# A two-block transformer layer on one core: barriers behind two attentions, and work that is moved among their items

## Chip, core and metric

The kernel runs on one core of one Trainium2 chip. The metric is the device time of one execution in microseconds, the median of the runs. The engines are called PE (TensorE, matrix products), DVE (VectorE), ACT (ScalarE), POOL (GpSimd) and SP (SyncE, which here only issues DMAs). ACTq and SPq in rows are the instruction queues of ACT and SP issuing DMAs.

## The reference

Two blocks run one behind the other on x of 512 rows (tokens) and 1024 columns. The first has a mixer (retention and a chunked RWKV-7 scan side by side), a cross-attention on 256 rows of memory, and an MLP. The second has four attentions on shares of the width, and a feed-forward with a convolution, all scaled and shifted by a vector c. Cut to what the change touches:

```python
x = x + y @ w_out                                    # y: retention and RWKV-7
x = x + memory_cross_attention(rmsnorm(x, norm_xattn), rmsnorm(mem, norm_mem), w_q, w_kv, w_o)
x = x + jnp.square(jax.nn.relu(h @ mlp_w_up)) @ mlp_w_down
x = rmsnorm(x, norm_final)
# second block; mod = silu(c) @ ada_w + ada_b, cut into sh_a, sc_a, gt_a, sh_m, sc_m, gt_m
h = rmsnorm_2(x, norm_mix_g) * (1.0 + sc_a) + sh_a
proj = h @ w_in
# o_a: diff attention, rmsnorm_2(o, sub_g) * (1 - lam_init) behind it; o_b: forgetting attention
# o_c: stick-breaking attention; o_d: sparse attention of three branches, whose keys
#      d_ks (selected) and d_kw (window) are columns of proj of 64 each
mixed = jnp.concatenate([o_a, o_b, o_c, o_d], axis=-1) @ w_out_2
x = x + gt_a * mixed
x = x + gt_m * conv_ffn(rmsnorm_2(x, norm_ffn_g) * (1.0 + sc_m) + sh_m, ...)
```

## The kernel before

Every large product is computed in three passes. A weight chunk of up to 128x2048 numbers is loaded by SP into one of two raw slots; ACT casts it to a rounded high part (line 409) and DVE subtracts that from the raw to get the low part (line 412), in one of two slots for parts; PE then multiplies high by high, high by low and low by high (line 389). The left side is split in the same way, into `AH` and `AL`. All weights of the program form one stream, `STREAM`. On every engine a generator walks over the chunks (`product_steps` on PE, `evac_steps` on ACT and DVE), and `fill(dense, n)` advances it by n units, a unit being half of a 128x512 block or one narrower block: 12 products of 512 columns. When `evac_steps` comes to a chunk it first splits the weights of the next one. The smaller work of a stage is written by hand between such fills, so each engine's order is fixed by the code and engines meet only at semaphores. `stage_end` is a barrier of PE, ACT and DVE.

The order of the stages: the start (parameters, norm of x), the first products `w_in` with rotation and retention among them (`front1_*`), the inversion of 64x64 triangles for the scan (`invert_*`), the scan, `w_out`, query and key products, cross-attention, `w_o`, the MLP, the second input product `w_in_2` with stick-breaking, the sparse branch's preparation and the norms of queries and keys among it (`front_*`), the mixers (40 items of the diff, forgetting and sparse attentions), sub-norm, `w_out_2`, and the feed-forward.

What the change touches:
- At the start, ACT squares x (`squares_act`, line 615), POOL makes the root (lines 624 and 626) and DVE scales the rows (line 631).
- `skew_bias_act` (line 548) issues eight DMAs of 512 KB from DRAM to DRAM, on ACT's queue, among the first products. What they write is read by `load_bias_act` at about 996 us.
- Cross-attention is a pipeline of 16 items over DVE, ACT and PE. Barriers stand before and behind it. Behind it `split_y_act` and `split_y_dve` (lines 737 and 742) split all of `yT` in four steps; the first two chunks of `w_o` wait for two each.
- `w_in_2` has 13 chunks. The key columns of the selected branch are multiplied twice side by side (they have to stand in both halves of the partitions), and so are those of the window branch, in a chunk of their own with 24 products.
- `norms_*` brings the sum of squares of the diff tiles first, and then that of the forgetting (fox) tiles.
- Behind the mixers stand a barrier, the sub-norm (`subnorm_*`), the rows of the two gates (`gate_rows_*`, 16 scalings on DVE and 16 products on PE), a barrier, and the split of all of `yT`.

## Time and profile before

| | us |
|---|---|
| median of 3 runs (1749.3 to 1753.15) | 1750.53 |
| profiled execution | 1750.18 |
| its span | 1748.0 |
| PE busy in it | 1645.3 |
| DVE, ACT, POOL busy | 902.6, 661.4, 72.7 |
| chain that ended last, share of PE | 82% |
| mean granted clock of PE | 0.976 |
| PE waits in line 647 for DVE's rows, four times | 13.8 |
| PE waits in line 389 for low weights, five times | 13.5 |
| PE waits in line 389 for the low part of `yT`, twice | 11.0 |
| PE waits in line 2202 for ACT's squares | 4.7 |
| PE waits in the sub-norm and gate rows | 6.1 |
| PE waits in line 908 for the rotation, about 95 us | 0.9 |

How to read the rows below. A row of the timeline has the start and the duration in us, the engine, the line of the code, the operation, the tiles written and read, the shape, the count, and in brackets how long the engine stood idle before it and what ended that. A matmul's duration overlaps the next one's, so its pace is read from starts. A granted clock of 1.00 is the higher level of PE's clock, 2.4 GHz, and 0.50 the lower, 1.2 GHz. A row of a window has its bounds, its length, busy time and count for PE, PE's weight loads, DVE, ACT and POOL, then the granted clock, the DMA engines' share and GB/s.

### The profile page before, as it was taken

To read this page: it belongs to the slowest core of one execution; us is meant where nothing else is said; L and a number is where in the kernel's file an instruction comes from. 1 tells how busy PE (TensorE), PEld (TensorE's weight loads), DVE (VectorE), ACT (ScalarE), POOL (GpSimd) and SP (SyncE) were. 2 spreads that over 40 slices of the span, in tenths; PEclk is the share of its full clock that TensorE was granted. 3 is DMA by queue.
4 is the path that set the end of the run, shared out by engine and by line. 5 is a ranking of instruction groups with operands and counts; after the bars stand their busy time and mean duration, and the time that the engine had idled before them with its cause. 6 is when DMAs were issued, how large, how long until landed. Compare 5 with 4: busy or idle time off the path is not lost.

```text
span 1748.0 us, 26094 instructions
## 1 busy us (share of the span) xinstructions
PE 1645.3 (94%) x11261; PEld 1321.4 (76%) x11261; DVE 902.6 (52%) x1405; ACT 661.4 (38%) x987; POOL 72.7 (4%) x105
## 2 busy tenths in 40 slices
PE   6899989999998999999999899889787999999998
PEld 5766769977895778888888687666456788888887
DVE  5354576526443454545454644326774555555544
ACT  4225831243434254232331443544772422222220
POOL 1200100000000000000000200001400000000000
PEclk9999999999999999999999999997998999999999
DMA  6912220002350344545444331320001233323322
GB/s 204 263 54 60 64 81 4 4 28 95 96 163 31 124 156 135 199 139 179 159 169 166 114 78 49 78 92 25 1 1 49 72 97 97 97 97 97 96 85 84
DMA packets 152260, 169.50 MB, mean 97 GB/s; under 512 B 16264, under 2 KB 113154, under 8 KB 151762
## 3 DMA queue, kind: packets, MB, share of 16 engines
q1 hardware_dynamic: 143128, 152.10, 27.6%
q10 hardware_dynamic: 9018, 15.74, 3.1%
q8 instruction: 89, 1.46, 0.4%
q14 instruction: 25, 0.20, 0.0%
HBM read 163.60 MB, written 6.32 MB: 97 GB/s over the span
## 4 chain that ended last, share of the span: by engine, by line
PE 82%; DVE 6%; ACT 6%; POOL 2%; issue 2%; ACTq 2%; DMA 1%; DVEq 0%; POOLq 0%
PE ps L389 65%; PE ps L1265 4%; PE ps L1424 2%; DVE weights_low L412 1%; PE ps L2359 1%; ACT weights_high L409 1%; PE ps L2532 1%; PE ps L2347 1%; PE ps L1644 1%; PE ps L2370 1%; ACT sb_hT L2448 1%; POOL sb_hT L2489 1%; PE ps L908 1%; PE ps L920 1%; PE ps L2202 1%
## 5 line engine op out<-in xcount | busy, mean ns | idle before, releaser
L389 PE MATMUL ps<-left_high,weights_high 128*128 128x512 f32 x1024 | 409.4, 400 | 20.3 <-DVE weights_low L412 13.5
L412 DVE TENSOR_TENSOR weights_low<-sb_weights_raw,weights_high 128x2048 fp32r<-128x2048 f32 (+2 forms) x119 | 266.5, 2239 | 285.0 <-ACT weights_high L409 284.9
L389 PE MATMUL ps<-left_high,weights_low 128*128 128x512 f32 x1024 | 401.6, 392 | 0.0
L389 PE MATMUL ps<-left_low,weights_high 128*128 128x512 f32 x1024 | 401.5, 392 | 0.0
L409 ACT CAST weights_high<-sb_weights_raw 128x2048 fp32r<-128x2048 f32 (+2 forms) x119 | 222.4, 1869 | 345.6 <-PE ps L389 301.3
L389 PEld LDWEIGHTS ps<-left_high,weights_high 128*128 128x128 f32 x1024 | 193.3, 189 | 75.8 <-DVE weights_low L412 18.3
L389 PEld LDWEIGHTS ps<-left_high,weights_low 128*128 128x128 f32 x1024 | 193.1, 189 | 41.8
L389 PEld LDWEIGHTS ps<-left_low,weights_high 128*128 128x128 f32 x1024 | 193.6, 189 | 41.1 <-issue 1.7
L389 PE MATMUL ps<-weights_high,hidden_high 128*128 128x512 f32 x432 | 169.0, 391 | 0.0
L389 PE MATMUL ps<-weights_high,hidden_low 128*128 128x512 f32 x432 | 168.2, 389 | 0.0
L389 PE MATMUL ps<-weights_low,hidden_high 128*128 128x512 f32 x432 | 168.1, 389 | 0.0
L389 PE MATMUL ps<-weights_high,left_high 128*128 128x512 f32 (+2 forms) x352 | 118.8, 337 | 11.7 <-DVE left_low L742 11.0
L389 PE MATMUL ps<-weights_low,left_high 128*128 128x512 f32 (+2 forms) x352 | 117.5, 334 | 0.0
L389 PE MATMUL ps<-weights_high,left_low 128*128 128x512 f32 (+2 forms) x352 | 117.5, 334 | 0.0
L389 PEld LDWEIGHTS ps<-weights_high,hidden_low 128*128 128x128 f32 x432 | 81.1, 188 | 17.1
L389 PEld LDWEIGHTS ps<-weights_low,hidden_high 128*128 128x128 f32 x432 | 81.1, 188 | 16.6
L389 PEld LDWEIGHTS ps<-weights_high,hidden_high 128*128 128x128 f32 x432 | 81.1, 188 | 16.6
L389 PEld LDWEIGHTS ps<-weights_high,left_high 128*128 128x128 f32 x352 | 67.6, 192 | 21.2 <-issue 13.2
L1843 DVE TENSOR_TENSOR hidden_low<-sb_arena,hidden_high 128x512 fp32r<-128x512 f32 x54 | 37.4, 692 | 89.5 <-ACT hidden_high L1838 89.5
L389 PEld LDWEIGHTS ps<-weights_low,left_high 128*128 128x128 f32 x352 | 67.6, 192 | 6.8 <-issue 0.2
L389 PEld LDWEIGHTS ps<-weights_high,left_low 128*128 128x128 f32 x352 | 67.6, 192 | 6.5
L1265 PE MATMUL ps<-sb_arena 64*64 64x64 f32 x2048 | 63.8, 222 | 5.0 <-DVE sb_arena L1316 4.1
(382 smaller groups left out, 2062.7 us busy)
## 6 DMA issues: line engine op xcount, KB each, us to landing
sb_weights_raw<-in_w_in SPq DMA_DIRECT2D x25, 1024.0 KB, 5.3
sb_yT<-in_ada_w SPq DMA_DIRECT2D x24, 1024.0 KB, 5.2
sb_weights_raw<-in_ffn_w_up SPq DMA_DIRECT2D x44, 512.0 KB, 5.1
sb_weights_raw<-in_mlp_w_up SPq DMA_DIRECT2D x16, 1024.0 KB, 6.3
sb_weights_raw<-in_mlp_w_down SPq DMA_DIRECT2D x16, 1024.0 KB, 7.6
sb_weights_raw<-in_ffn_w_down SPq DMA_DIRECT2D x10, 1024.0 KB, 5.0
sb_weights_raw<-in_w_out SPq DMA_DIRECT2D x8, 1024.0 KB, 5.0
sb_weights_raw<-in_xattn_w_kv SPq DMA_DIRECT2D x8, 1024.0 KB, 5.1
```

What stands on the lines that cost most here:

```text
L389: last = nc.tensor.matmul(o, lhsT, rhs, start=b["first"] and i == 0, stop=b["last"] and i == len(pairs) - 1)
L409: nc.scalar.copy(h[:, 0:n], raw[:, 0:n]).then_inc(w_high, 1)
L412: nc.vector.tensor_tensor(l[:, 0:n], raw[:, 0:n], h[:, 0:n].bitcast(F32), ALU.subtract).then_inc(w_low, 1)
L908: nc.tensor.matmul(ps[:, 2 + n % 4, 0:w], KTt[b, p_, kt * P:(kt + 1) * P], QT[b, p_, kt * P:S], start=True, stop=True).then_inc(ret_scores, 1)
L920: last = nc.tensor.matmul(ps[64 * e:64 * e + 64, 6 + p_ % 2, kt * P:S], VR[:, kt, h * 64:(h + 1) * 64], SCO[:, (s - 2) % 3, e, 0:w], start ...
L1265: last = nc.tensor.matmul(ps[b, bank, c * 64:(c + 1) * 64], lhsT(b, u, c), rhs(b, u, c), start=True, stop=True)
L1424: last = nc.tensor.matmul(o_of(b), *own_pairs[i], start=i == 0, stop=i == len(own_pairs) - 1)
L1644: last = nc.tensor.matmul(ps[b, 6 + o % 2, q0:S], v_of(x), PT[0:m, buf, x, q0:S], start=grp["begins"] and x == 0, stop=grp["ends"] and x = ...
L1843: nc.vector.tensor_tensor(HIDL[part % 2][:, i, :], x, HIDH[part % 2][:, i, :].bitcast(F32), ALU.subtract).then_inc(ff_low, 1)
L2202: last = nc.tensor.matmul(ps[:, 2 + f, :], mat, SQ[:, f, :], start=True, stop=True)
L2347: nc.tensor.matmul(ps[:, j % 4, 0:it["w"]], l, r, start=True, stop=True).then_inc(mx_scores, 1)
L2359: last = nc.tensor.transpose(ps[0:m, 4 + e, i * P:(i + 1) * P], src[:, c0:c0 + m], ident)
```

## The change

- The squares of the first norm are computed by DVE; the loop is staggered by one tile.
- The eight bias DMAs are issued at the head of `invert_act` instead of among the first products. Several semaphores are merged; the waits keep their meaning.
- The barrier behind cross-attention is gone. `yT` is split by tile of 128x512 beside the items (`CROSS_SPLIT`), and `w_o` goes in halves of the contracted dimension: both column chunks of tiles 0 to 3, then both of tiles 4 to 7, with all eight banks of PSUM open.
- The keys of both branches come from one product of 128 columns; ACT copies the two halves apart, and two DMAs copy each into the other half of the partitions. The chunk of 24 products is gone; the fox chunks now come ahead of the diff chunks, and the norm sums are in that order too.
- The gate rows are turned by two transposes in `sparse_pe`, stored in DRAM and loaded back with a broadcast.
- Both barriers behind the mixers are gone. Four tiles of `yT` are split beside items 10, 12, 17 and 21; the square of the diff outputs stands at item 20, its two sums on PE at items 35 and 38, and the rest of sub-norm beside the first half of `w_out_2`, which takes tiles 2 to 5 first and then 6, 7, 0, 1.

```diff
+        def squares_dve(v, nm, t):
+            o = nm["at"] + t
+            nc.vector.tensor_tensor_reduce(out=nm["rows"][:, t, :], in0=nm["src"][:, t, :], in1=nm["src"][:, t, :],
+                                           scale=1.0, scalar=0.0, op0=ALU.mult, op1=ALU.add,
+                                           accum_out=stat[:, o:o + 1]).then_inc(squares_done, 1)
...
             swap_act(a, 0)
-            skew_bias_act(a)
...
         def invert_act(a):
-            a.eng.dma_start(GUP0, A["rwkv_g_up"][0, 0:P]).then_inc(gate_up_loaded, 16)
-            a.eng.dma_start(GUP1[0:32], A["rwkv_g_up"][0, P:P + 32]).then_inc(gate_up_loaded, 16)
+            a.eng.dma_start(GUP0, A["rwkv_g_up"][0, 0:P]).then_inc(front_loaded, 16)
+            a.eng.dma_start(GUP1[0:32], A["rwkv_g_up"][0, P:P + 32]).then_inc(front_loaded, 16)
+            skew_bias_act(a)
...
+        def in_halves(W, halves, rows_of, evac_of):
+
+            out_ = []
+            for half in halves:
+                for c0 in (0, 512):
+                    blocks = [by_token(0, 512, lambda k, t=t, half=half: rows_of(t)(half[k]), "dve", evac_of(t, c0), nk=4,
+                                       first=half is halves[0], last=half is halves[-1]) for t in range(NT)]
+                    runs = [half] if half[3] - half[0] == 3 else [half[0:2], half[2:4]]
+                    out_.append(dict(pieces=[kview(W)[:, r[0]:r[-1] + 1, c0:c0 + 512] for r in runs], nk=4, width=512,
+                                     blocks=blocks, by_k=len(runs) > 1))
+                out_[-2]["left"] = 4
+            return out_
+
+        def add_half(t, c0):
...
+                if n in beside:
+                    split_low_dve(v, beside[n])
...
+                if n in beside:
+                    a.wait_ge(sa_out_kept, base_out + beside[n] + 1)
+                    split_high_act(a, beside[n])
...
+        def split_high_act(a, k):
+            nc.scalar.copy(AH[:, k, :], yT[:, k, :]).then_inc(split_high, 1)
+
+        def split_low_dve(v, k):
+            v.wait_ge(split_high, v.count(split_high))
+            nc.vector.tensor_tensor(AL[:, k, :], yT[:, k, :], AH[:, k, :].bitcast(F32), ALU.subtract).then_inc(split_low, 1)
+
+        CROSS_SPLIT = {8: 0, 9: 1, 12: 2, 13: 3, 16: 4, 17: 5}
...
+        def two_keys(a, src, free, value):
+
+            upper, lower = slice(0, 64), slice(64, P)
+            nc.scalar.copy(QK[upper, 10, :], src[upper])
+            nc.scalar.copy(QK[lower, 11, :], src[lower]).then_inc(free, 1)
+            a.wait_ge(free, value)
+            a.eng.dma_start(QK[lower, 10, :], QK[upper, 10, :]).then_inc(keys_spread, 16)
+            a.eng.dma_start(QK[upper, 11, :], QK[lower, 11, :]).then_inc(keys_spread, 16)
...
-            chunk_of(w2((2564, 2692), (2692, 2756), (2692, 2756)), [
-                by_feature(0, P, h_tile, S, "act", act_copy_to(KV)), fcol(P, 10)]),
+            chunk_of(w2((2564, 2692), (2692, 2756), (2820, 2884)), [
+                by_feature(0, P, h_tile, S, "act", act_copy_to(KV)), by_feature(P, P, h_tile, S, "act", two_keys)]),
             chunk_of(w2((2756, 2820), (2884, 2960), (1536, 1540)), trow(0, 144, 768)),
             chunk_of(w2((2308, 2564)), [fcol(0, 8), fcol(P, 9)]),
-            chunk_of(w2((2820, 2884), (2820, 2884)), [fcol(0, 11)]),
-
+
+            chunk_of(w2((1024, 1280)), [fcol(0, 6), fcol(P, 7)]),
+            chunk_of(w2((768, 1024)), [fcol(0, 4), fcol(P, 5)]),
             chunk_of(w2((0, 256)), [fcol(0, 0), fcol(P, 1)]),
             chunk_of(w2((256, 512)), [fcol(0, 2), fcol(P, 3)]),
-            chunk_of(w2((768, 1024)), [fcol(0, 4), fcol(P, 5)]),
-            chunk_of(w2((1024, 1280)), [fcol(0, 6), fcol(P, 7)]),
             chunk_of(w2((512, 768)), trow(0, 256, 0)),
             chunk_of(w2((1280, 1536)), trow(0, 256, 256)),
         ]
@@ -2063,11 +2080,11 @@
...
-            columns_kept(a, 6)
+            store_gates_act(a)
+            columns_kept(a, 5)
...
+            for i, (tiles, SQ, n, kept) in enumerate(((QK[:, 4:8, :], SQ_FOX, 64, 7), (QK[:, 0:4, :], SQ_DIFF, 32, 9))):
+                columns_kept(a, kept)
+                if i == 0:
+                    a.wait_ge(nsa_normed, 2)
+                nc.scalar.activation(SQ, tiles, ACT.Square).then_inc(qk_squared, 1)
+                fill(dense, 3 - i)
+                nc.scalar.preload_act_table_set(LN_SET)
+                a.wait_ge(qk_sums, 2 + i)
+                nc.scalar.activation(SQ, ps[:, 2:6, :], ACT.Ln, bias=EPS6, scale=1.0 / n).then_inc(qk_ln, 1)
+                nc.scalar.preload_act_table_set(EXP_SET)
+                a.wait_ge(qk_ln, 2 + i)
+                nc.scalar.activation(SQ, SQ, ACT.Exp, scale=-0.5).then_inc(qk_rstd, 1)
...
+            split_weights(a, "act", w_in_2[6]["index"])
...
-        def subnorm_pe(pe):
-            pe.wait_ge(qk_squared, 4)
-            for f in range(2):
-                last = nc.tensor.matmul(ps[:, f, :], sum64, DSQ[:, f, :], start=True, stop=True)
-            last.then_inc(qk_sums, 1)
-            gate_rows_pe(pe, DIAG, 6)
-            gate_rows_pe(pe, DIAG_M, 4)
-
...
+        def turn_gates_pe(pe):
+
+            for i, m in enumerate((16, 40)):
+                nc.tensor.transpose(ps[0:KT, 6, 64 + i * P:64 + (i + 1) * P], MOD[:, m:m + KT], ident)
+
+        def keep_gates_dve(v):
+            nc.vector.tensor_copy(GATE_ROWS, ps[0:KT, 6, 64:64 + 2 * P]).then_inc(gate_rows, 1)
+
...
+        def load_gates_act(a, i):
+            a.wait_ge(gate_moved, 32)
+            a.eng.dma_start((GROW, GROW_M)[i], gate_dram[i:i + 1].to_broadcast([P, D])).then_inc(gate_moved, 16)
...
+        MIX_SPLIT = {10: 4, 12: 5, 17: 2, 21: 3}
+
+        def beside_mixers_act(a, n):
+
+            if n in MIX_SPLIT:
+                k = MIX_SPLIT[n]
+                if k < 4:
+                    a.wait_ge(mx_out_kept, k + 1)
+                nc.scalar.copy(Y_HIGH[:, k - 2, :], yT[:, k, :]).then_inc(split_high, 1)
+            if n == 20:
+                a.wait_ge(fox_bias, 2 * len(FOX_ITEMS))
+                a.wait_ge(mx_out_kept, 2)
+                nc.scalar.activation(DSQ, yT[:, 0:2, :], ACT.Square).then_inc(qk_squared, 1)
+                load_gates_act(a, 0)
+            if n in (36, 39):
+                f = (n - 36) // 3
+                a.wait_ge(qk_sums, 4 + f)
+                nc.scalar.copy(DSQ[:, f, :], ps[:, 6, :]).then_inc(qk_ln, 1)
+
+        def beside_mixers_pe(pe, n):
+            if n in (35, 38):
+                f = (n - 35) // 3
+                pe.wait_ge(qk_squared, 4)
+                pe.wait_ge(mx_out_kept, 5)
+                if f:
+                    pe.wait_ge(qk_ln, 4)
+                nc.tensor.matmul(ps[:, 6, :], sum64, DSQ[:, f, :], start=True, stop=True).then_inc(qk_sums, 1)
+
+        def beside_mixers_dve(v, n):
+            if n in MIX_SPLIT:
+                k = MIX_SPLIT[n]
+                v.wait_ge(split_high, v.count(split_high))
+                nc.vector.tensor_tensor(Y_LOW[:, k - 2, :], yT[:, k, :], Y_HIGH[:, k - 2, :].bitcast(F32),
+                                        ALU.subtract).then_inc(split_low, 1)
+
+        TMPG = view(4096, 512)
...
+        def mixed_rows_2(t):
+            tok = slice(t * P, (t + 1) * P)
+            return lambda k: (Y_HIGH[:, k - 2, tok], Y_LOW[:, k - 2, tok]) if 2 <= k < 6 else \
+                (AH[:, k, tok], AL[:, k, tok])
+
+        w_out_2 = in_halves(A["w_out_2"][0], ((2, 3, 4, 5), (6, 7, 0, 1)), mixed_rows_2, gated_a)
...
-            for t in range(NT):
-                a.wait_ge(x_loaded[t // 2], 16)
-                squares_act(a, NORM_1, t)
...
         def w_o_pe(pe):
-            closing_norm_pe(pe, product_steps(pe, w_o, 8), w_o, NORM_4)
+            dense = product_steps(pe, w_o, 8)
+            for s in (sa_shifted, sa_kept):
+                pe.wait_ge(s, pe.seen[s.name])
+            fill(dense, 12)
+            pe.wait_ge(sa_out_kept, pe.seen[sa_out_kept.name])
+            closing_norm_pe(pe, dense, w_o, NORM_4)
...
         def w_out_2_act(a):
-            closing_norm_act(a, evac_steps(a, "act", w_out_2), w_out_2, NORM_6, gated)
+            dense = evac_steps(a, "act", w_out_2)
+            fill(dense, 1)
+            load_gates_act(a, 1)
+            a.wait_ge(mx_out_kept, 6)
+            for k in (6, 7):
+                split_high_act(a, k)
+            nc.scalar.preload_act_table_set(LN_SET)
+            a.wait_ge(qk_ln, 5)
+            nc.scalar.activation(DSQ, DSQ, ACT.Ln, bias=EPS6, scale=1.0 / HD).then_inc(act_order, 1)
+            nc.scalar.preload_act_table_set(EXP_SET)
+            a.wait_ge(act_order, a.count(act_order))
+            nc.scalar.activation(DSQ, DSQ, ACT.Exp, scale=-0.5).then_inc(qk_rstd, 1)
+            for k in (0, 1):
+                a.wait_ge(sub_normed, k + 1)
+                split_high_act(a, k)
+            closing_norm_act(a, dense, w_out_2, NORM_6, gated)
             nc.scalar.preload_act_table_set(SILU_SET)
...
             mixers_pe(pe)
-            pe.stage_end()
-            subnorm_pe(pe)
-            pe.stage_end()
             w_out_2_pe(pe)
             pe_products(pe, ffn)
```

The order of ACT's instructions where the bias DMAs stood, before: the load of `in_ret_masks`, the four DMAs of the first swap (line 863), and behind them the split of the fourth chunk's weights.

```order
L470 COPY sb_arena<-ps 128x512
L1166 DMA sb_yT<-in_ret_masks 128x4096
L863 DMA sb_arena<-sb_arena 32x2048 x4
L548 DMA bias_skewed<-bias_vectors 128x1024 x8
L409 CAST weights_high<-sb_weights_raw 128x2048
L470 COPY sb_arena<-ps 128x512 x2
```

And at the start of the inversion, before; the four copies keep the first products of the inversion:

```order
L1203 ACTIVATE sb_arena<-sb_arena 32x512
L1292 DMA sb_hT<-in_rwkv_g_up 128x512
L1293 DMA sb_hT<-in_rwkv_g_up 32x512
L1296 COPY sb_arena<-ps 128x512 x4
L1301 COPY sb_arena<-ps 128x512 x20
```

The same two places after the change, first among the first products, then at the inversion.

```order
L472 COPY sb_arena<-ps 128x512
L1152 DMA sb_yT<-in_ret_masks 128x4096
L849 DMA sb_arena<-sb_arena 32x2048 x4
L409 CAST weights_high<-sb_weights_raw 128x2048
L472 COPY sb_arena<-ps 128x512 x2
L409 CAST weights_high<-sb_weights_raw 128x2048
```

```order
L1188 ACTIVATE sb_arena<-sb_arena 32x512
L1277 DMA sb_hT<-in_rwkv_g_up 128x512
L1278 DMA sb_hT<-in_rwkv_g_up 32x512
L549 DMA bias_skewed<-bias_vectors 128x1024 x8
L1282 COPY sb_arena<-ps 128x512 x4
L1287 COPY sb_arena<-ps 128x512 x20
```

The eight DMAs went from the place ahead of the weight split to the place ahead of the inversion's first copy.

PE behind its last mixer product (line 2370 before, 2389 after), before and after:

```order
L2359 MATMUL ps<-sb_consts,sb_hT 128x128 x4
L2370 MATMUL ps<-sb_hT,sb_arena 64x128 x8
L2695 MATMUL ps<-sb_arena,sb_consts 128x512 x2
L2681 MATMUL ps<-sb_arena,sb_consts 128x128 x16
L389 MATMUL ps<-weights_high,left_high 128x512
L389 MATMUL ps<-weights_low,left_high 128x512
L389 MATMUL ps<-weights_high,left_low 128x512
```

```order
L2378 MATMUL ps<-sb_consts,sb_hT 128x128 x4
L2389 MATMUL ps<-sb_hT,sb_arena 64x128 x8
L389 MATMUL ps<-weights_high,mixed_high 128x512
L389 MATMUL ps<-weights_low,mixed_high 128x512
L389 MATMUL ps<-weights_high,mixed_low 128x512
L389 MATMUL ps<-weights_high,mixed_high 128x512
```

The two sums now stand among the last items, the sixteen gate products are gone, and the first products read the tiles split among the items.

ACT in `w_in_2`, from the table load behind the logarithms of stick-breaking's second pair; `in_nsa_phi_w` is the load of the compression weights, and `128x1280` are exponentials, before and after:

```order
L2601 ACT_TABLE_LOAD
L409 CAST weights_high<-sb_weights_raw 128x1024
L470 COPY sb_arena<-ps 128x512 x2
L2578 ACTIVATE sb_arena<-sb_arena 128x1280
L2606 DMA sb_yT<-in_nsa_phi_w 64x32x64 x2
L409 CAST weights_high<-sb_weights_raw 128x2048
L2578 ACTIVATE sb_arena<-sb_arena 128x1280
L470 COPY sb_arena<-ps 128x512
L409 CAST weights_high<-sb_weights_raw 128x2048
```

```order
L2623 ACT_TABLE_LOAD
L409 CAST weights_high<-sb_weights_raw 128x2048
L472 COPY sb_arena<-ps 128x512 x2
L2600 ACTIVATE sb_arena<-sb_arena 128x1280
L2629 DMA sb_yT<-in_nsa_phi_w 64x32x64 x2
L409 CAST weights_high<-sb_weights_raw 128x2048
L2600 ACTIVATE sb_arena<-sb_arena 128x1280
L472 COPY sb_arena<-ps 128x512
L2604 COPY sb_yT<-ps 128x512
```

The first cast belongs to the chunk that PE works on next: the short one of 1024 columns before, a full one now. The cast behind the DMAs is that of the chunk behind it in both, and the cast that followed the copy comes later.

## Rows read from the trace of the kernel before

**Rows 1.** Page of before, part 1: busy us of each engine
```profile
PE 1645.3 (94%) x11261; PEld 1321.4 (76%) x11261; DVE 902.6 (52%) x1405; ACT 661.4 (38%) x987; POOL 72.7 (4%) x105
```

**Rows 2.** Timeline of PE at the start of `w_o`: start, duration, engine
```profile
570.85 0.51 PE L389 MATMUL ps<-weights_high,left_high 128*128 128x512 f32 x1 [4.83 <-DVE left_low L742]
...
574.80 0.40 PE L389 MATMUL ps<-weights_low,left_high 128*128 128x512 f32 x1
...
580.25 0.39 PE L389 MATMUL ps<-weights_low,left_high 128*128 128x512 f32 x1
```

**Rows 3.** Timeline of the first 22 us, and the x loads by line
```profile
10.93 1.06 ACT L615 ACTIVATE sb_arena<-sb_X 128x1024 f32<-128x1024 f32 x1 [8.28 <-issue]
...
17.44 0.75 DVE L631 TENSOR_SCALAR sb_arena<-sb_X,sb_stat 128x1024 f32<-128x1024 f32 x1 [0.71 <-POOL sb_stat L626]
...
21.20 0.47 PE L389 MATMUL ps<-left_high,weights_high 128*128 128x512 f32 x1 [1.55 <-DVE left_low L675]
...
L554 SPq DMA_DIRECT2D sb_X<-in_x x2: 422/442/463, 1.2 to 1.6; - x2
...
DMA to landing us min/median/max: 5.4/6.5/7.6
```

**Rows 4.** Line 881 on POOL (ns min/median/max), and one of its rows beside DVE
```profile
L881 POOL TENSOR_TENSOR sb_arena<-sb_arena x8: 1286/1476/3267, 46.3 to 90.7; 128x512 f32<-128x512 f32 x8
...
65.45 2.28 DVE L412 TENSOR_TENSOR weights_low<-sb_weights_raw,weights_high 128x2048 fp32r<-128x2048 f32 x1
...
65.60 3.27 POOL L881 TENSOR_TENSOR sb_arena<-sb_arena 128x512 f32<-128x512 f32 x1 [0.63 <-DVE sb_arena L871]
```

**Rows 5.** Timeline from 49 to 62 us, and one window (clock 0.56)
```profile
49.73 7.77 ACTq L548 DMA_DIRECT2D bias_skewed<-bias_vectors  x8
57.60 1.90 ACT L409 CAST weights_high<-sb_weights_raw 128x2048 fp32r<-128x2048 f32 x1 [11.34 <-issue]
...
61.88 0.79 PE L389 MATMUL ps<-left_high,weights_high 128*128 128x512 f32 x1 [5.36 <-DVE weights_low L412]
...
61.90:66.50 4.60, 4.60 (x12) 3.64 (x13) 4.39 (x5) 0.37 (x1) 2.56 (x2) 0.56 1.04 282
```

**Rows 6.** The bias DMAs' issues (ns min/median/max), and the inversion's first rows
```profile
L548 ACTq DMA_DIRECT2D bias_skewed<-bias_vectors x8: 505/664/1652, 49.7 to 56.9; - x8
...
55.52 1.98 ACTq L548 DMA_DIRECT2D bias_skewed<-bias_vectors  x3
...
250.48 0.45 ACTq L1293 DMA_DIRECT2D sb_hT<-in_rwkv_g_up  x1
252.01 0.58 ACT L1296 COPY sb_arena<-ps 128x512 f32<-128x512 f32 x1 [2.63 <-PE ps L1265]
...
252.72 0.69 DVE L1307 TENSOR_TENSOR sb_arena<-ps,sb_consts 128x512 f32<-128x512 f32 x1 [2.70 <-ACT sb_arena L1296]
```

**Rows 7.** Timeline of `w_in_2` with stick-breaking and norm sums
```profile
1091.90 1.97 ACTq L2606 DMA_DIRECT2D sb_yT<-in_nsa_phi_w  x2
...
1095.78 1.26 ACT L2578 ACTIVATE sb_arena<-sb_arena 128x1280 f32<-128x1280 f32 x1
...
1098.25 0.80 PE L389 MATMUL ps<-left_high,weights_high 128*128 128x512 f32 x1 [6.14 <-DVE weights_low L412]
1103.67 2.37 PE L2541 MATMUL ps<-sb_arena 128*64 128x512 f32 x16
...
1112.07 3.59 PE L2092 MATMUL ps<-sb_arena,sb_consts 128*128 128x512 f32 x8
...
1168.44 5.40 PE L2202 MATMUL ps<-sb_arena,sb_consts 128*128 128x512 f32 x8 [4.69 <-ACT sb_arena L2214]
```

**Rows 8.** Timeline behind the mixers, and the window of their last 78 us
```profile
1307.93 0.58 ACT L2463 COPY sb_yT<-ps 128x512 f32<-128x512 f32 x1 [0.76 <-PE ps L2370]
...
1329.31 0.76 PE L389 MATMUL ps<-weights_high,left_high 128*128 128x512 f32 x1 [6.12 <-DVE left_low L742]
...
1230.00:1308.00 78.00, 66.12 (x570) 40.97 (x566) 55.98 (x244) 57.57 (x210) 19.16 (x24) 0.98 0.01 2
```

223 lines of the change are left out of this document (99 added, 124 removed).

## The prediction

> **What bounds the kernel now.** I read the page first, then the waits of TensorE (PE), then the timeline round each long wait. PE is busy for 1645.3 of the 1748.0 us [rows 1], and most of that is the product loop of line 389, which issues a 128x512 product every 0.227 us at full clock, 2.4 GHz ((580.25 - 574.80) / 24), and about every 0.44 us with the clock at its lower level, 1.2 GHz: right behind a stall, from 570.85 to 574.80, ten took 3.95 us instead of 2.27 [rows 2]. So the span can shrink in three ways only: fewer PE instructions, shorter PE waits, less PE work at half clock. Work of VectorE (DVE), ScalarE (ACT) or the queues counts only where PE ends up waiting. Each term below is therefore a shift of PE's own timeline; the next product chunk follows behind every one of them, and apart from the places named the waits between are small.
>
> The span is 1748.0 us and the profiled execution 1750.18 us, so 2.2 us lie outside; the median of the runs, 1750.53, is the same within 0.02%. I subtract from 1750.2.
>
> **The start: squares on DVE.** Before, ACT issues the parameter loads first and squares x only from 10.93 us; four tiles of x later DVE ends at 18.19 and the first product starts at 21.20. The two halves of x were issued at 1.2 and 1.6 and landed after 5.4 and 7.6 us, at 6.6 and 9.2 [rows 3]. DVE's squares have no row; the nearest is its fused 128x512 operation, and by the step between sizes I estimate 1.2 us for 1024 elements. Four squares and four scalings from 6.6 us then end at about 15.0, 3.2 us earlier. But the chain goes through GpSimd (POOL), and POOL's 128x512 operation took 3.27 us beside a DVE subtraction that reads two tiles of SBUF, against 1.29 at its shortest [rows 4]. If POOL's two small operations of a tile are held in the same way while DVE squares the next one, a tile takes some 2.6 us instead of the 1.47 before, the rows end near 17.3 and 0.9 us is left. The Trainium skill, SBUF — State Buffer, section Who interferes with whom, says that a DVE instruction with two SBUF inputs contends with a GpSimd instruction that reads SBUF; by that rule alone the term would be -0.9, without it -3.2. Those rows of POOL agree with the rule. The bounds are -0.5 and -3.2; nearer to the blocked end I take **-1.5 us**.
>
> **Bias vectors: eight DMAs moved from the first products to the inversion.** ACT spends 7.77 us (49.73 to 57.50) issuing the eight `bias_skewed` DMAs; the weight split behind them starts only at 57.60, and PE stands 5.36 us until 61.88. Then it works at a granted clock of 0.56 over the next 4.6 us [rows 5]: nine products at 0.44 instead of 0.227, 1.9 us. A 0.9 us wait of the retention's first scores on the rotation (the DMAs of the swap share the queue with these eight) should go as well. The weights themselves had landed long before, so once ACT is free nothing is late next: split 1.9, subtraction 2.3, ready about 3 us before PE asks. Gain 8.2 us, at least 6.
>
> They are now issued at the head of `invert_act`, behind two gate loads that end at 250.93, and ahead of ACT's first copy at 252.01, which DVE awaits 0.1 us later [rows 6]. From there DVE runs its masks without a gap for 14 us, and PE waits for the last of them, so what delays the copy delays the stage one for one. One issue took 0.505, 0.664 or 1.652 us (least, median, most) [rows 6]; the last three, with the queue drained of the swap, took 1.98 together, 0.66 each. Eight of these are 5.3 us; ACT is free at 256.2, 4.2 us late. Bounds: eight at 0.505, 2.9 us, and the whole 7.77, 6.7 us. PE also sits idle longer and may do more of the next level at half clock, up to 2 us. I take **+4.5 us** (2.9 to 9). Together the move is worth **-3.7**.
>
> **Cross-attention to w_o: no barrier, halves.** PE's last attention product ends at 566.0; it stands 4.83 us, until the split of the first two tiles of yT (ACT, then DVE), and its first ten products take 1.7 us longer than at full pace [rows 2]: 6.5 us in all. After the change tiles 0 to 3 are split at items 8, 9, 12 and 13, the weights of the first chunk are ready as before, and 96 products (21.8 us) of the first half run before tiles 4 to 7 are needed, of which the last two take ACT and DVE some 5 us with the next weight split. So nothing is late next. Cost: one 0.6 us cast now stands ahead of ACT's last copy of turned weights, and the casts beside items 8 to 13 fall where DVE and ACT are mostly idle: 0.6. **-5.3 us** (3.5 to 6.5).
>
> **w_in_2: one chunk less, another order.** Removed: 24 products, 24 x 0.227 = 5.4 us. The order matters more. Before, the short dup chunk ends at 1092.1, and the next chunk's split stands on ACT behind two DMA issues that themselves wait for DVE's exponents; PE waits 6.14 us and then needs 5.4 us for 12 products that should take 2.7 [rows 7]. After the change the chunk at that place is a full one, so PE has 24 more products ready. It now reaches the stick-breaking times_v at 1094.8 and waits there for ACT's exponentials, which come behind the same two issues and the same split and end at 1097.05 [rows 7]: a new wait of 2.4 us, where before it got there at 1103.67. Net 6.4 us. Second, the sums of the norms: PE waited 4.69 us for the fox squares, which ACT reached only behind Ln of the diff tiles, a table load and a split, and ran the eight rows in 5.40 us instead of 3.59 [rows 7]: 6.5 us. Now both squares are placed right behind their columns, three units of products (8 us) ahead of PE's use, against 4.4 us of ACT work, so that wait goes. Two small waits of 0.3 and 0.2 shrink. Added on PE: two 8x128 transposes, 0.3. The two half-copies and two DMA issues of the shared product lie in ACT's idle time before the exponentials (4.3 us there); the gate stores cost ACT under 1 us, with PE's products ahead. Sum: 5.4 + 6.4 + 6.5 + 0.2 - 0.3 = **-18.2 us** (13 to 21).
>
> **Mixers to w_out_2: barriers, sub-norm and gate rows.** PE's last mixer product ends at 1307.9 and the first product of w_out_2 starts at 1329.31 [rows 8]: 21.4 us in which PE did 36 instructions of sums and gate rows. The first seven products run at half clock, 1.4 us more. After the change the four tiles of the first half are split by item 21, and PE goes on at once. The next things due are the second weight split (ready about 5 us after the last item, wanted after 10.9), the broadcast of the gate row (wanted after 24 us), and sub-norm with its two table loads, two functions, scaling and splits (some 12 us, wanted after 21.8). None is late, so the whole 22.8 us go.
>
> What is put in among the items costs something: PE gets two f32 128x512 sums, 0.9 each at full clock (3.59 / 4 [rows 7]); ACT gets four casts of 0.6, one square of 1.06 and two copies of 0.6; DVE four subtractions of 0.7. From 1230 on PE is busy 66 of 78 us, DVE 56 and ACT 58 [rows 8], each waiting for another by turns, so cover is thin. A split also ties DVE to ACT once, since the subtraction waits for a cast that stands behind ACT's copies; I estimate 1 us for each of the four (those at items 10 and 12 lie partly under POOL's bias work). 4 x 1 + 1.8 + 1 for the rest is nearly 7, less what is hidden: 6 us. Bounds 2 (the PE sums alone) and 12 (all of it serial, 1.8 + 4.7 + 2.8, and 2.7 of coupling). **-16.8 us** (11 to 21).
>
> **Sum.** -1.5 - 3.7 - 5.3 - 18.2 - 16.8 = -45.5, so 1750.2 - 45.5 = **1704.7 us**.
>
> **Rivals.**
> A. Waits come back in another place: the issues of the DMAs cost the inversion 9 us and DVE and ACT are coupled in the mixers for 12. For it: ACT stands directly on the chain at 252.01, and cover in the mixers is thin. Against: the issues were long only behind the swap. 1704.7 + 4.5 + 6 = 1715.2. Chance 0.2.
> B. The upper ends hold: starts at -3.2, inversion +2.9, mixers +2, front -20: 1704.7 - 1.7 - 1.6 - 4 - 1.8 = 1695.6. Chance 0.15.
> C. The change doesn't do what it says at w_out_2: the second waits put in (bank of the sums, kept outputs) or the first chunk's weights stop PE for as long as sub-norm takes. The order shows the products right behind the last times_v, and the first chunk's weights were there before the mixers, so this is unlikely. 1704.7 + 15 = 1719.7. Chance 0.06.
> D. The other side: half clock through the mixers. PE's clock was at its lower level for part of their first third. If waits among the items held it there from 1230 us to the end, the 66 us of PE work would take 0.44 / 0.227 as long, 62 us more: 1704.7 + 62 = 1767, slower than before. It decides once 74% of that stretch (46 us over 62) is at half clock. Against: the stretch is now granted 0.98 [rows 8], and two sums make PE fuller, not emptier. Chance 0.02.
> My forecast has 0.57.
>
> **The numbers.** The predicted time is that of the forecast, 1704.7. A measurement of this kernel can tell 0.2%, 3.5 us, from no change. A range for 8 in 10 takes in B and A with their neighbours: 1693 to 1719. Faster 0.97, same 0.01, slower 0.02.
>
> **What the profile after would show.** First product near 19.7 us, not 21.2; no wait of PE at the fourth chunk of w_in; ACT's first copy of the inversion some 4 us behind PE's gram products; w_o's first product right behind the last attention product; one wait of 2 to 3 us at the stick-breaking times_v and none at the norm sums; the first w_out_2 product right behind the last mixer product and a mixer stage 2 to 12 us longer. PE busy about 20 us lower. I am wrong if the inversion's copy is more than 7 us late, if DVE or ACT is the releaser of long PE waits in the mixers, or if a new wait on low weights stands in w_in_2.

## The result, and the profile after

The changed kernel took 1733.30 us, the median of four runs (1730.08 to 1741.98), against 1749.91 before. The ratio is 0.9905, 95% interval 0.9882 to 0.9928: 0.95% faster, where 1704.7 was forecast and 1693 to 1719 was the range. The direction was right, the size was not: 16.6 us instead of 45.5.

The profiled execution is the fastest of the four, 1730.08 us with a span of 1728.1, so the trace explains 19.9 us (1748.0 - 1728.1), and 3.2 us of the median lie outside it; an experiment below shows where. Part 1 of the page after, PE's line, against [rows 1]:

```profile
PE 1633.0 (95%) x11207; PEld 1313.1 (76%) x11207; DVE 903.3 (52%) x1404; ACT 660.5 (38%) x990; POOL 75.9 (4%) x105
```

PE's busy time fell by 12.3 us (about 20 were forecast), so only 7.6 of the 19.9 us gained are idle time, though waits of 5.4, 4.8, 6.1 and 4.7 us and two barriers were to go. To see where the rest stayed, I cut both timelines of PE at the first instruction of each stage. All are starts of PE rows, in us of the stage:

| stage, from its first PE product to the next one's | before | after | difference | forecast |
|---|---|---|---|---|
| start, up to the first product | 21.20 | 19.27 | -1.93 | -1.5 |
| first products, up to the inversion (rotation, retention) | 228.91 | 228.35 | -0.56 | -8.2 |
| inversion and scan, up to `w_out` | 133.14 | 138.56 | +5.42 | +4.5 |
| `w_out`, queries and keys of cross-attention | 144.86 | 144.86 | 0.00 | 0 |
| cross-attention, up to its last eight products | 32.51 | 36.46 | +3.95 | +0.6 |
| those products and `w_o`, up to the MLP | 61.26 | 54.61 | -6.65 | -5.9 |
| MLP and the norm behind it | 369.44 | 369.42 | -0.02 | 0 |
| `w_in_2` up to stick-breaking's second times_v | 112.35 | 105.78 | -6.57 | -6.4 |
| from there up to the mixers | 91.07 | 94.17 | +3.10 | -11.8 |
| mixers (before: with sub-norm and gate rows) | 134.57 | 119.44 | -15.13 | -15.4 |
| `w_out_2`, up to the feed-forward | 52.13 | 50.72 | -1.41 | -1.4 |
| feed-forward | 366.56 | 366.46 | -0.10 | 0 |

Two rows hold nearly the whole miss: the first products (7.6 us short) and the stretch from times_v to the mixers (14.9 us short). Cross-attention adds 3.4.

**The first products.** Against [rows 5] the weight split is no longer late; two other waits stand there. PE's timeline (columns as in that of before):

```profile
67.24 0.39 PE L389 MATMUL ps<-weights_high,left_high 128*128 128x256 f32 x1 [1.77 <-DVE weights_low L412]
...
77.42 0.58 PE L389 MATMUL ps<-weights_high,left_high 128*128 128x256 f32 x1 [4.16 <-ACT sb_arena L472]
```

ACT's timeline, with the casts, the second swap's issues and the copy:

```profile
47.26 1.91 ACT L409 CAST weights_high<-sb_weights_raw 128x2048 fp32r<-128x2048 f32 x1 [2.92 <-issue]
...
72.08 3.02 ACTq L849 DMA_DIRECT2D sb_arena<-sb_arena  x4
75.19 1.90 ACT L409 CAST weights_high<-sb_weights_raw 128x2048 fp32r<-128x2048 f32 x1 [9.10 <-issue]
77.00 0.64 ACT L472 COPY sb_arena<-ps 128x256 f32<-128x256 f32 x2
```

DVE's, with the first and last rotation row of the first swap and the weight subtraction between:

```profile
61.20 0.69 DVE L854 TENSOR_TENSOR sb_arena<-sb_arena 128x512 f32<-128x512 f32 x1 [9.70 <-DMA sb_arena<-sb_arena]
...
64.91 2.28 DVE L412 TENSOR_TENSOR weights_low<-sb_weights_raw,weights_high 128x2048 fp32r<-128x2048 f32 x1
...
70.39 1.60 DVE L857 TENSOR_TENSOR sb_arena<-sb_arena 128x512 f32<-128x512 f32 x1
```

The four DMAs of the first swap by line (what ACT spent on one issue in ns, the first and last start in us, the time to landing), after the change and before it:

```profile
L849 ACTq DMA_DIRECT2D sb_arena<-sb_arena x4: 612/614/860, 44.4 to 46.5; - x4
...
DMA to landing us min/median/max: 10.2/11.1/14.6
```

```profile
L863 ACTq DMA_DIRECT2D sb_arena<-sb_arena x4: 612/670/1025, 46.3 to 48.8; - x4
...
DMA to landing us min/median/max: 10.1/11.1/13.0
```

ACT now casts at 47.26 instead of 57.60. But DVE, free at 51.5, stands 9.70 us for the swapped tiles, whose DMAs were issued from 44.4 and landed only at 61. The next weight subtraction stands behind that rotation (64.91), which is PE's wait of 1.77 us; the second swap waits for the end of the rotation (72.0), ACT's copy that frees PE's bank stands behind it (77.00), and that is the wait of 4.16 us. Behind it, PE works some 6 us at half pace. Before, the last of the four landed 13.0 us after its issue at 48.8, so at 61.7, and DVE came free from the late split at 61.8: the landing was just as late as the split, and hidden by it.

**From times_v to the mixers.** The wait of 4.69 us of [rows 7] is gone; both sums start without one. A longer one stands further on. PE's timeline:

```profile
1176.82 0.55 PE L389 MATMUL ps<-weights_high,left_high 128*128 128x256 f32 x1 [11.74 <-DVE sb_arena L475]
```

ACT's, from the square of the diff tiles over the cast to the logarithm and the exponential:

```profile
1152.44 1.93 ACT L2233 ACTIVATE sb_yT<-sb_arena 128x2048 f32<-128x2048 f32 x1
1165.17 1.90 ACT L409 CAST weights_high<-sb_weights_raw 128x2048 fp32r<-128x2048 f32 x1 [10.80 <-PE ps L389]
...
1168.38 1.97 ACT L2237 ACTIVATE sb_yT<-ps,sb_eps 128x2048 f32<-128x2048 f32 x1
...
1171.66 1.91 ACT L2240 ACTIVATE sb_yT<-sb_yT 128x2048 f32<-128x2048 f32 x1
```

DVE's, with bank copies (line 475) and the scaling of the diff tiles (line 2248):

```profile
1155.16 0.75 DVE L475 COPY sb_arena<-ps 128x256 f32<-128x256 f32 x2
...
1173.60 1.41 DVE L2248 SCALAR_TENSOR_TENSOR sb_arena<-sb_arena,sb_derived_cols,sb_yT 128x512 f32<-128x512 f32 x2 [17.69 <-ACT sb_yT L2240]
1174.93 1.41 DVE L2248 SCALAR_TENSOR_TENSOR sb_arena<-sb_arena,sb_param_cols,sb_yT 128x512 f32<-128x512 f32 x2
1176.26 0.75 DVE L475 COPY sb_arena<-ps 128x256 f32<-128x256 f32 x2
```

The sums of the diff tiles are done at 1162.2. ACT doesn't take them, because its next instruction is the cast of the next weights, which waits 10.80 us, until PE at 1165.1 has used up the slot. The logarithm, the table load and the exponential follow, DVE's scaling waits for them 17.69 us, and DVE's two copies, which give PE its banks back, stand behind the scaling. PE, with two banks for its products here, has run out of them at 1165.1. The clock is at its lower level from 1168.5 to 1182.2, so the products of the first 5.3 us behind the wait run at half pace.

**What went as forecast.** times_v waits 2.27 us (2.4 forecast); no wait stands at the weights of the fourth chunk or at the norm sums; `w_o` and `w_out_2` start right behind their attentions, the latter at 1310.92, 18.4 us earlier than in [rows 8]:

```profile
1310.92 0.50 PE L389 MATMUL ps<-weights_high,mixed_high 128*128 128x512 f32 x1
```

### The profile page after: what moved, and what is told of

It reads as the page before. It is cut to its first block, busy times and chain, and to the rows that moved or that the text cites. A ratio compares the mean times of both kernels' runs of the same rounds, so it can differ in the third digit from the quotient of the medians.

```text
span 1728.1 us, 25989 instructions
## 1 busy us (share of the span) xinstructions
PE 1633.0 (95%) x11207; PEld 1313.1 (76%) x11207; DVE 903.3 (52%) x1404; ACT 660.5 (38%) x990; POOL 75.9 (4%) x105
## 4 chain that ended last, share of the span: by engine, by line
PE 82%; ACT 6%; DVE 6%; issue 2%; POOL 2%; ACTq 1%; DMA 1%; DVEq 0%; POOLq 0%; SPq 0%
PE ps L389 65%; PE ps L1250 4%; PE ps L1410 2%; PE ps L2378 1%; DVE weights_low L412 1%; ACT sb_hT L2469 1%; PE ps L2554 1%; PE ps L1636 1%; ACT weights_high L409 1%; PE ps L2366 1%; DMA sb_arena<-sb_arena 1%; PE ps L2389 1%; PE ps L894 1%; PE ps L906 1%; PE ps L381 0%
## 5 line engine op out<-in xcount | busy, mean ns | idle before, releaser
L389 PE MATMUL ps<-left_high,weights_high 128*128 128x512 f32 (+1 forms) x1016 | 404.1, 398 | 7.4 <-DVE left_low L693 3.2
L412 DVE TENSOR_TENSOR weights_low<-sb_weights_raw,weights_high 128x2048 fp32r<-128x2048 f32 (+1 forms) x118 | 265.3, 2248 | 263.1 <-ACT weights_high L409 263.1
L389 PE MATMUL ps<-left_low,weights_high 128*128 128x512 f32 (+1 forms) x1016 | 396.9, 391 | 0.0
L389 PE MATMUL ps<-left_high,weights_low 128*128 128x512 f32 (+1 forms) x1016 | 396.6, 390 | 0.0
L409 ACT CAST weights_high<-sb_weights_raw 128x2048 fp32r<-128x2048 f32 (+1 forms) x118 | 221.5, 1877 | 349.5 <-PE ps L389 294.1
L389 PEld LDWEIGHTS ps<-left_high,weights_high 128*128 128x128 f32 (+1 forms) x1016 | 190.6, 188 | 60.9 <-issue 13.7
L389 PEld LDWEIGHTS ps<-left_high,weights_low 128*128 128x128 f32 (+1 forms) x1016 | 190.8, 188 | 41.4
L389 PEld LDWEIGHTS ps<-left_low,weights_high 128*128 128x128 f32 (+1 forms) x1016 | 190.9, 188 | 40.4 <-issue 1.7
L389 PE MATMUL ps<-weights_high,left_high 128*128 128x256 f32 (+2 forms) x320 | 107.8, 337 | 19.4 <-DVE sb_arena L475 13.1
L389 PE MATMUL ps<-weights_low,left_high 128*128 128x256 f32 (+2 forms) x320 | 106.1, 331 | 0.0
L389 PEld LDWEIGHTS ps<-weights_low,hidden_high 128*128 128x128 f32 x432 | 81.1, 188 | 16.6
L389 PEld LDWEIGHTS ps<-weights_high,hidden_high 128*128 128x128 f32 x432 | 81.1, 188 | 16.5
L389 PEld LDWEIGHTS ps<-weights_high,left_high 128*128 128x128 f32 x320 | 63.2, 198 | 27.3 <-issue 12.6
```

What stands on the lines that cost most here:

```text
L389: last = nc.tensor.matmul(o, lhsT, rhs, start=b["first"] and i == 0, stop=b["last"] and i == len(pairs) - 1)
L409: nc.scalar.copy(h[:, 0:n], raw[:, 0:n]).then_inc(w_high, 1)
L412: nc.vector.tensor_tensor(l[:, 0:n], raw[:, 0:n], h[:, 0:n].bitcast(F32), ALU.subtract).then_inc(w_low, 1)
```

## The experiments

Each is the changed kernel with one thing altered, unless said otherwise. Medians of these kernels scatter by 3 us for a reason that the run of the unaltered kernel shows, so where a stage is at stake I read its length in the trace. Diffs are against the changed kernel. Five of the expectations also give a span, counted from the first trace of the changed kernel, and all five came out 3.5 to 11 us too low: 6.4 to 6.6 us of each miss lie in the mixers, which those edits don't touch.

### The swap ahead of the masks

```diff
-            a.eng.dma_start(DECAY, A["ret_masks"]).then_inc(front_loaded, 16)
             swap_act(a, 0)
+            a.eng.dma_start(DECAY, A["ret_masks"]).then_inc(front_loaded, 16)
```

> The changed kernel with one step moved: ACT issues the four DMAs of the first swap ahead of the 2 MB load of the retention masks instead of behind it. Theory 1 (the swapped tiles land late because they stand behind 2 MB on the same queue, and DVE's rotation, which waits for them, holds the weight subtraction and the second swap): the swap lands within 8 us instead of 11 to 15, DVE's rotation starts near 53 us instead of 61.2, PE's waits of 1.77 us (67.2) and 4.16 us (77.4) go, with 1.5 us of half clock behind the second, so the first product of line 990 comes 6 to 7.5 us earlier than at 168.0 and the span is near 1721. Rival (the swap is slow because the weight loads of SP take the DMA engines): landing stays over 11 us, and the gain is under 1 us.

Measured: 1728.88 us, ratio 0.988 (0.9865 to 0.9895). The first product of line 990 (the RWKV-7 branch, later in the same stage) came at 161.02 instead of 167.98, and no wait over 0.8 us stands between the first product and it. The landing of the first swap by line:

```profile
L849 ACTq DMA_DIRECT2D sb_arena<-sb_arena x4: 613/616/1187, 45.9 to 47.8; - x4
...
DMA to landing us min/median/max: 3.1/4.1/4.9
```

And the first row of DVE's rotation in the timeline, now without a wait:

```profile
54.49 0.69 DVE L854 TENSOR_TENSOR sb_arena<-sb_arena 128x512 f32<-128x512 f32 x1
```

The slowest of the four landed after 4.9 us instead of 14.6. The rival, SP's weight loads, falls with the next two runs, which have the bias DMAs back and differ in this order alone: SP issued no load in either between 39.1 and 59.7 us, and the four landed after 10.1 to 12.7 us behind the 2 MB load and after 3.1 to 5.0 ahead of it. So the 2 MB load ahead of the swap on the same queue was the cause, and theory 1 holds; only the last 2 us or so of the 14.6, where SP issued a load at 51.5, are not separated. The Trainium skill, DMA: Bandwidth & Descriptors, section Queues, rings and completion order, says that on each DMA engine the descriptors of one queue are consumed in ring order; the runs agree, 14.6 against 4.9 us. It is no order of landing: in the changed kernel the 2 MB load landed at 55.3 us, and the first of the four DMAs behind it at 54.6.

### The bias DMAs back among the first products

```diff
             swap_act(a, 0)
+            skew_bias_act(a)
             fill(dense, 8)
...
-            skew_bias_act(a)
             for u in range(NPAIR):
```

> The changed kernel with the eight bias DMAs issued where the kernel before had them, behind the first swap among the first products. Theory 3 (the move was worth almost nothing at the first products, because the rotation behind the landing of the swap was late right behind the weight split, and cost 5.4 us at the inversion): PE's 5.4 us wait for the fourth chunk's weights is back, but the first product of line 990 comes within 1 us of 168.0, the inversion's DVE masks start 5.4 us earlier behind its first product, and the span is 5 us shorter, about 1723. Rival (as predicted blind: 8.2 us gained at the first products against 5.4 at the inversion): 2.8 us longer, about 1731.

Measured: 1732.99 us, ratio 0.9889 (0.9867 to 0.9911). Both theories were wrong in part. The first product of line 990 came at 172.90, so the move was worth 4.9 us there, not under 1 and not 8.2; the inversion was 133.13 us, 5.4 shorter, as both said. The two cancel: the first mixer product comes at 1191.09 against 1191.48. The kernel before, with the same order of the DMAs, lost less: from the first product to that of line 990 it took 148.88 us, this run 153.70. The second row below has a part of it: the second swap, whose DMAs landed after 6.0 to 11.6 us (4.6 to 8.9 before; the bias DMAs, which there landed up to 76.5 us, stand ahead of it), lets DVE start at 88.15 instead of 86.44, and PE's wait for the rotation is 3.14 us instead of 0.86. PE also had 10.2 us at the lower clock level in this stage against 6.8. What is left of the 4.8 us is open.

PE's timeline:

```profile
61.16 0.57 PE L389 MATMUL ps<-left_high,weights_high 128*128 128x512 f32 x1 [4.99 <-DVE weights_low L412]
...
97.89 1.13 PE L894 MATMUL ps<-sb_arena 64*128 64x512 f32 x4 [3.14 <-DVE sb_arena L857]
```

### The swap ahead, and the bias DMAs back

```diff
-            a.eng.dma_start(DECAY, A["ret_masks"]).then_inc(front_loaded, 16)
             swap_act(a, 0)
+            a.eng.dma_start(DECAY, A["ret_masks"]).then_inc(front_loaded, 16)
+            skew_bias_act(a)
...
-            skew_bias_act(a)
             for u in range(NPAIR):
```

> As e1_swap_ahead_of_masks, but with the eight bias DMAs issued among the first products again, behind the swap and the masks. Theory 3: with the swap out of the way, the price of the eight issues at that place is what the forecast took for it, 7 to 8.5 us to the first product of line 990 (161.0 in e1, so 168 to 169.5), while in the changed kernel, where the swap was late, it was 4.9 (168.0 against 172.9). Rival (ACT's split was never the cause): under 4 us. The inversion is 5 to 6 us shorter in either case, so the span is within 3 us of that of e1.

Measured: 1732.11 us from two runs, ratio 0.9892 (0.9867 to 0.9918). The product of line 990 came at 167.99, 6.97 us after that of the run with the swap ahead alone; PE's wait for the split is there (5.27 us), and none for the rotation. So the forecast's 8.2 us was nearly the right price for the eight issues at that place, but it could be earned only once the swap was out of the way. The inversion took 134.06 us, 5.0 shorter.

### The bias DMAs where ACT waits anyway

```diff
             for f in range(4):
                 fill(dense, 1)
                 decays_act(a, f)
+            for f in range(4):
+                fill(dense, 1)
+                skew_bias_act(a, (2 * f, 2 * f + 1))
             fill(dense, 62)
...
-            skew_bias_act(a)
             for u in range(NPAIR):
```

> The changed kernel with the eight bias DMAs issued in pairs behind four of the last products of the first stage (about 215 to 240 us), where ACT waits 4 to 6 us for PE between its copies, instead of at the head of the inversion. Theory 3: the inversion stage (first product of line 1250 at its start to the first product of w_out) is 5.4 us shorter, 133.1 instead of 138.6, and nothing is longer before it; the span falls by 5.4. Rival (4 MB of DRAM traffic or the issues delay a weight chunk, PE waits for weights near 230 us): the stage before grows by 1 us or more.

Measured: 1727.65 us, ratio 0.9872 (0.9845 to 0.9898). The issues fell between 215.8 and 221.3 us, ahead of a wait of ACT for PE of 3.8 us; the stretch they are in, from line 990 to the inversion, kept its 79.6 us, and the inversion stage went from 138.56 to 134.31. That is 4.3 of the 5.4 us; ACT's first copy is as early as before, but PE had 12.9 us at the lower clock level in that stage against 10.2 before. The rival is out.

### The chain of the diff norms, on ACT alone and on both engines

```diff
-                fill(dense, 3 - i)
+                fill(dense, 3 if i == 0 else 0)
...
-                fill(dense, 5 if i == 0 else 0)
+                fill(dense, 5 if i == 0 else 2)
```

The second kernel has in `norms_dve` also `fill(dense, 4 - 2 * i)` for `fill(dense, 2)`.

> The changed kernel with one step moved on ACT: the two units of products that stood between the square of the diff tiles and the logarithm of their sums now stand behind the exponential. Theory 2 (PE's wait of 11.74 us at 1176.8 is the root chain of the diff norms: ACT waits 10.8 us for PE to free the weight slot, with the cast ahead of the logarithm; DVE's scaling waits for ACT, and the bank copies that PE needs stand behind the scaling): the logarithm starts right behind the sums at about 1162.3, DVE's scaling ends near 1170, and PE's wait falls from 11.7 to 4 to 6 us; span 1721 to 1723. Rival (the bank copies are late for DVE's own reasons, or the cast moved back becomes the new wait): PE's wait stays within 2 us of 11.7, or a wait as long appears at the first product of w_out_2.

> As e2_norm_act, and DVE takes two more units (four instead of two) between the scaling of the fox tiles and that of the diff tiles. Theory 2: PE now has two more banks to write while the chain of the diff norms runs (5.8 us of products), so no wait over 1 us is left before the mixers; the stage gives 13 us (the two waits of 1.3 and 11.7) and about 1 us of half clock, span 1714 to 1716. If the waits were only moved, the first mixer product comes less than 8 us earlier than at 1191.5.

Measured: 1727.97 us, ratio 0.9874 (0.9859 to 0.9888), and 1725.43, ratio 0.9857 (0.9841 to 0.9873). In the first, the logarithm in ACT's timeline and PE's wait:

```profile
1161.45 1.97 ACT L2237 ACTIVATE sb_yT<-ps,sb_eps 128x2048 f32<-128x2048 f32 x1 [6.58 <-PE ps L2224]
```

```profile
1169.90 0.55 PE L389 MATMUL ps<-weights_high,left_high 128*128 128x256 f32 x1 [5.62 <-DVE sb_arena L475]
```

PE's wait in the second:

```profile
1174.23 0.39 PE L389 MATMUL ps<-weights_high,left_high 128*128 128x256 f32 x1 [1.97 <-DVE sb_arena L475]
```

The wait fell from 11.74 to 5.62 and to 1.97 us, and the stage from 94.17 to 87.18 and 85.12. So both links are shown: the cast ahead of the logarithm, and the bank copies behind the scaling. Of the 13 us expected 9 came: waits of 1.30 and 1.97 us are left, since DVE's subtraction of the next weights also stands ahead of the copies, and here PE had half clock behind times_v.

### The subtractions one item later, in both attentions

```diff
-            attention_dve(v, cross, SRX, {n: k for n, k in CROSS_SPLIT.items() if n <= 16})
+            attention_dve(v, cross, SRX, {n + (n < 16): k for n, k in CROSS_SPLIT.items() if n <= 16})
```

> The changed kernel with DVE's four subtractions for tiles 0 to 3 of yT in cross-attention one item later than ACT's casts (items 9, 10, 13 and 14 instead of 8, 9, 12 and 13). Theory 4 (the attention stage grew from 32.5 to 36.5 us because each subtraction makes DVE wait 1.0 to 1.6 us for a cast that stands behind ACT's copies, and the next item's probabilities come late by that): DVE's waits for the casts go, the two PE waits of 1.82 us shrink below 0.8 us, and the stage from the first product of line 1613 to the last of line 1636 is 2 to 3 us shorter. Rival (the work put in is itself too much for ACT, four casts of 0.6 us): no more than 0.7 us.

Measured: 1728.47 us, ratio 0.9876 (0.9856 to 0.9895). The stage took 34.07 us instead of 36.46, and what was waited for in it (total, times, longest) in the changed kernel and in this one:

```profile
DVE left_low L1803 <- ACT left_high L1799: 6.7, 5, 1.6
PE ps L1624 <- DVE sb_arena L1690: 4.9, 5, 1.8
```

```profile
DVE left_low L1803 <- ACT left_high L1799: 1.9, 3, 1.5
PE ps L1624 <- DVE sb_arena L1690: 1.3, 3, 0.8
```

The price of the splits in cross-attention was 3.95 us, and 2.4 of it was the tie of DVE to ACT. The same edit in the mixers:

```diff
-            if n in MIX_SPLIT:
-                k = MIX_SPLIT[n]
+            if n - 1 in MIX_SPLIT:
+                k = MIX_SPLIT[n - 1]
```

> The changed kernel with DVE's four subtractions among the mixers one item later than ACT's casts. The stage (first mixer product to first product of w_out_2) was 119.4 us in the profiled run of the changed kernel and 125.8 to 125.9 in four of its variants, with more of it at the lower clock level. Theory 4: each subtraction costs DVE a wait of 1.3 us as at 1258.9, so the stage is 2 to 4 us shorter at the same clock pattern (about 122.5 where it would be 125.8). Rival (the cost is the casts and sums themselves): under 1 us.

Measured: 1732.36 us, ratio 0.9884 (0.9863 to 0.9906); the stage 122.75 us, granted clock 0.83. Kernels with the mixers unaltered had 124.7 us at 0.85 and 125.8 to 126.0 at 0.81 (below), so 0.83 would be near 125.3, and the edit is worth some 2.5 us by an estimate that leans on the clock. The best version, with this edit, had 117.9 at 0.90 against the changed kernel's 119.4 at 0.89; some 1.1 of these 1.6 us go to the clock by the slope of 6.6 us for 0.08 (below), and 0.5 is left. So the edit is worth 0.5 to 2.5 us by estimate. What the trace does show is that the waits are gone. DVE's subtractions and what they waited for in the changed kernel:

```profile
L2747 DVE TENSOR_TENSOR mixed_low<-sb_yT,mixed_high x4: 692/693/746, 1239.7 to 1270.0; 128x512 fp32r<-128x512 f32 x4
...
  ACT mixed_high L2723: 4.4, 4
```

Four waits, 4.4 us in total; with the edit there is none. How much of that reached PE is not settled.

### The changed kernel once more

> The changed kernel itself, unaltered, once more. Its runs lay between 1730.1 and 1742.0, and the stage from the first mixer product to w_out_2 was 119.4 us in its profile but 125.8 to 126.0 in five variants that touch nothing there. Theory 5 (the clock that the mixers are granted varies from run to run; the first profile caught a favourable one): the stage is over 122 us in this profile, with more than 27 us of it at the lower level, and the median stays at 1731 to 1735. Rival (the variants' edits upstream cause it): 119.4 again, with 27 us at the lower level.

Measured: 1736.97 us (1732.34 to 1737.90), ratio 0.9915 (0.9894 to 0.9936). The mixers in before (to their last product, without sub-norm), in the first profile of the changed kernel, and in this one (window, length, busy time and count of PE, its weight loads, DVE, ACT and POOL, granted clock, DMA):

```profile
1194.70:1308.00 113.30, 96.67 (x728) 59.30 (x728) 80.91 (x336) 80.06 (x282) 26.57 (x32) 0.89 0.01 1
```

```profile
1191.50:1310.90 119.40, 100.43 (x732) 61.03 (x732) 83.98 (x340) 83.85 (x288) 26.66 (x32) 0.89 0.02 6
```

```profile
1193.00:1319.00 126.00, 108.59 (x733) 66.50 (x733) 83.87 (x340) 84.00 (x288) 26.98 (x32) 0.81 0.02 5
```

Same instructions, same busy time of DVE and ACT, 6.6 us longer, at a granted clock of 0.81 instead of 0.89. PE was granted the lower level for 47.8 us of this stretch against 27.3. So the clock of this stage is not fixed by the program. The stage came out as theory 5 expected. The median didn't: 1736.97 us against an expected 1731 to 1735. The eight runs of this kernel lie between 1730.08 and 1741.98 us. Of the nine profiles in which nothing in the stage was altered, six had 0.81 and 125.8 to 126.0 us; the others had 0.85 (124.7), 0.87 (121.3) and 0.89 (119.4). The first trace was the most favourable of the nine, and the 3.2 us between it and the median are of this size and kind. What tips it is not shown. Nor is it shown whether the change has a part in it: of before there is one trace, at 0.89, but 29 of its 32 runs lie between 1747.7 and 1752.3 us, closer together than those of the changed kernel.

### All edits together

> All edits together: the swap ahead of the masks, both steps of the norms, the later subtractions in both attentions, the bias DMAs behind the last products of the first stage. If the theories hold and the gains add: 7 + 9 + 3 + 5.4 + 2 = 26 us under the 1733 of the changed kernel's median, 1703 to 1709. If they only move the waits, over 1715.

Measured: 1703.40 us, ratio 0.9725 (0.9708 to 0.9741). The gains add. Cumulative in the trace (of the slowest run, 1710.39 us, with the mixers at 0.83): the inversion starts 8.1 us earlier than in the changed kernel, `w_out` 13.0, cross-attention's end 15.4, the mixers 22.6.

One more step, in stick-breaking:

```diff
             weights(1, 0)
-            for i in range(2):
-                a.wait_ge(st_arg, 4)
-                a.eng.dma_start(PHI[...], ...).then_inc(prep_loaded, 16)
-            fill(dense, 1)
             weights(1, 1)
+            fill(dense, 1)
+            for i in range(2):
+                a.wait_ge(st_arg, 4)
+                a.eng.dma_start(PHI[...], ...).then_inc(prep_loaded, 16)
```

> As e8_all, and in the stick-breaking attention ACT takes the second exponential of the second pair at once, then the cast of the next weights, and then issues the two loads of the compression weights, which stood ahead of both. Theory 6 (PE's wait of 2.4 us at line 2563 is two DMA issues and a cast ahead of an exponential whose input is ready): the wait goes, the stage from w_in_2 to that product is 103.5 us instead of 106.1, and 1.5 us of half clock behind it goes too; median 1699 to 1701. Rival (the cast or the loads become late): the wait stays at over 1 us in another line within 20 us, 1703.

Measured: **1701.11 us** (1698.80 to 1706.09), ratio 0.9722 (0.9695 to 0.9749), the lowest median here. The runs overlap with those of the version above (1702.11 to 1710.39), so what the step is worth is read from the trace: the wait at times_v is gone, and the stage took 103.48 us instead of 106.08. The stretch behind it took 82.09 instead of 85.27, with no time at the lower clock level instead of 6.8 us.

### The splits behind the mixers

On the version above, `w_out_2_dve` having its four subtractions at its head likewise:

```diff
-        MIX_SPLIT = {10: 4, 12: 5, 17: 2, 21: 3}
+        MIX_SPLIT = {}
+        MIX_TILES = (4, 5, 2, 3)
...
         def w_out_2_act(a):
             dense = evac_steps(a, "act", w_out_2)
+            for k in MIX_TILES:
+                nc.scalar.copy(Y_HIGH[:, k - 2, :], yT[:, k, :]).then_inc(split_high, 1)
```

> As e10_all_and_stick, but the four casts and four subtractions of the split stand behind the mixers, ahead of the first half of w_out_2, and not among the items. What stays among them are the square, two sums, their two copies. Forecast's price (1 us for each of the four splits, 1.8 for the sums): first to last mixer product 4 us less than the 117.9 of e10 at the same clock reading of 0.90 (113.9; at a reading of 0.81 6.5 us more), and then a wait of PE of about 4 us for the splits: four casts of 0.6, the last subtraction and the next weight split. Rival (the splits hide among the items and the sums on PE are the price): the mixers are less than 1.5 us shorter.

Measured: 1703.48 us, ratio 0.9742 (0.9723 to 0.9762). The mixers with and without the splits, and PE's wait behind them:

```profile
1163.30:1281.20 117.90, 99.55 (x732) 59.69 (x732) 84.05 (x340) 83.37 (x288) 26.41 (x32) 0.90 0.02 6
```

```profile
1159.20:1276.40 117.20, 101.39 (x732) 61.64 (x732) 80.67 (x336) 81.55 (x284) 26.29 (x32) 0.87 0.02 6
```

```profile
1280.15 0.47 PE L389 MATMUL ps<-weights_high,mixed_high 128*128 128x512 f32 x1 [3.78 <-issue]
```

0.7 us shorter as it stands, but at a clock reading of 0.87 instead of 0.90. By the slope of the pair above (6.6 us for 0.08) that is 2.5 us, so by this estimate the splits cost about 3 us among the items, between the 4 of the forecast and the rival's 1.5. They save the wait of 3.78 us behind them, for which the profile names no releaser; ACT's four casts and DVE's four subtractions stand there, up to 1280.1 us. In the medians (1703.48 and 1701.11 us, with runs that overlap) the two places are level.

## Why the prediction was wrong, step by step

In the trace 25.6 us of the forecast's 45.5 are missing: 7.6 at the first products, 14.9 between times_v and the mixers, 3.4 in cross-attention; the other stages came within 1 us each.

**Start: right.** 1.93 us came where 1.5 (0.5 to 3.2) was forecast. What decided it is POOL's root, which takes 1.4 us beside DVE's squares and 0.55 without them. POOL's timeline, then DVE's squares:

```profile
8.78 0.55 POOL L633 TENSOR_TENSOR sb_stat<-sb_stat,sb_eps 128x1 f32<-128x1 f32 x1
...
10.25 1.42 POOL L633 TENSOR_TENSOR sb_stat<-sb_stat,sb_eps 128x1 f32<-128x1 f32 x1
...
12.59 1.41 POOL L633 TENSOR_TENSOR sb_stat<-sb_stat,sb_eps 128x1 f32<-128x1 f32 x1
```

```profile
10.04 1.22 DVE L621 CUSTOM_DVE_ANT_0 sb_arena<-sb_X 128x1024 f32<-128x1024 f32 x1
...
12.37 1.22 DVE L621 CUSTOM_DVE_ANT_0 sb_arena<-sb_X 128x1024 f32<-128x1024 f32 x1
```

A tile takes 2.3 us while squares are left (10.25 to 12.59), near the 2.6 that the forecast had for the blocked case, and a square took 1.22, as estimated. The rule of the Trainium skill, SBUF — State Buffer, section Who interferes with whom, holds here: a DVE instruction with both inputs in SBUF (here the same tile) delayed one of GpSimd that reads SBUF, by 0.87 us (1.42 - 0.55).

**Bias DMAs at the first products: the step "once ACT is free nothing is late next" failed.** The forecast asked only whether the weights had landed. It looked past DVE, where the subtraction stands behind a rotation that waits for the swap. The row was there to be found, in the trace of before: its first swap landed up to 13.0 us after the issue, the last of it at 61.7 us, as late as the stall that was to go. The late landing and the second swap behind it took 7.6 of the 8.2 us. With the swap ahead, 7.0 us came back.

**Inversion: right.** The eight issues took 5.99 us (5.3 forecast, 4.0 to 7.8 the bounds). The 0.66 us for one was read from issues "with the queue drained of the swap", which it wasn't: they fell at 55.5 to 56.9, and the swap landed up to 61.7. ACT's copies and DVE's masks followed:

```profile
248.46 5.99 ACTq L549 DMA_DIRECT2D bias_skewed<-bias_vectors  x8
254.49 2.05 ACT L1282 COPY sb_arena<-ps 128x512 f32<-128x512 f32 x4 [7.61 <-PE ps L1250]
```

```profile
255.21 0.69 DVE L1293 TENSOR_TENSOR sb_arena<-ps,sb_consts 128x512 f32<-128x512 f32 x1 [7.68 <-ACT sb_arena L1282]
```

ACT's copy came 6.9 us behind the stage's first product instead of 1.9, so 5.0 late (4.2 forecast). The stage lost 5.4 us for a forecast 4.5. The sum of the move was -3.7 in the forecast and +4.9 in fact.

**Cross-attention and w_o: the gain right, the cost mis-sized.** The forecast names one cost of 0.6 against a gain of 6.5, which makes -5.9; its -5.3 follows only if 0.6 is taken twice, for the cast ahead of the last copy and for those beside the items, and so the table has it. 6.65 us were gained at the end against 5.9. What was put in cost 3.95 us instead of 0.6. The term looked at how idle ACT and DVE are, and not at the order: a subtraction that waits for a cast holds DVE's next item. The forecast had named that tie in the mixers and priced it there at 1 us each; it was left out here.

**w_in_2: right up to times_v** (6.57 against 6.4, its wait 2.27 against 2.4), **and wrong behind it.** The step that failed is "that wait goes", with no question of what is late next. Only the squares were followed to PE. The chain goes on through the sums, the logarithm, the exponential and the scaling to DVE's queue, on which PE's bank copies stand. In the changed order a cast that waits for PE stands within that chain. Waits of 13.1 us (11.74 and 1.31), and half clock behind them, took more than the 6.5 and the 5.4 us that the removed wait and the removed products had given. The run with both edits gave 9 us of it back, the best version 12, some 3 of them by the clock.

**Mixers and w_out_2: right at this trace's clock, with luck in it.** 16.5 us against 16.8; what was put in cost 6.1 us (119.4 - 113.3, at the same clock reading of 0.89) for a forecast of 6. The last runs put about 3 of it on the splits. Rival D named the clock in this stretch as the danger, with half clock to its end; what happened was a smaller form of it, 6.6 us in six of nine profiles. In those the stretch was 12.7 us longer than in the one trace of before (126.0 - 113.3), beyond the forecast's bound of 12; that the first trace gave 6.1 was luck.

**The rivals and the range.** Rival A had waits coming back in the inversion and the mixers, up to 1715; they came back in the first products and behind the norm sums, which no rival covered. The range was built from the uncertainty of durations. The error was in two places where a wait was struck out without the next one being followed on every queue, and there both terms were taken at their full size. The signs of being wrong that the forecast named didn't cover them either: the inversion's copy was 5.0 us late (up to 7 allowed), the longest wait of PE in the mixers was 2.35 us (2.25 before), and no new wait on low weights stands in `w_in_2`.

## What to carry to other kernels

When a stall goes, its size is not the gain: follow each engine's in-order queue from the freed instruction on, and ask for every wait on it (a DMA's landing too) when it would end without the stall; where the old stall hides the answer, ask the trace when the DMA landed. A norm's chain is late or early by its last consumer, not by its first operation. Where one engine's work waits for another's within a pipeline, put the second an item later. Small urgent DMAs go ahead of a large one on a queue.

## What the runs showed of the hardware

- Four DMAs of 256 KB each from SBUF to SBUF, issued behind a 2 MB load on the same queue, landed after 10.2 to 14.6 us, and after 3.1 to 4.9 when they were issued ahead of it; with eight DMAs of 512 KB behind both, 10.1 to 12.7 against 3.1 to 5.0.
- The same program was granted 0.89 or 0.81 of PE's clock over the same 120 us, 6.6 us apart, with the same instructions and the same busy time of DVE and ACT. A profile of one execution can therefore be off by 0.4% of this kernel. Differences below that between two variants should be read from stages, or from stretches at the same clock reading.
- Of eight issues of DRAM-to-DRAM DMAs the total was 7.77, 7.49 and 6.69 us behind the swap (before, and the two runs with them back at the old place), and 5.99 and 5.90 us at the inversion, behind two small loads (the changed kernel, and the run with the swap ahead).
